# One expert load of 1 MB issued as sixteen transfers of eight partitions

## What is computed

```python
def expert_block(args):
    xb, e = args
    return (jax.nn.silu(xb @ w1[e]) * (xb @ w3[e])) @ w2[e]
```

## Time and profile before

| | |
|---|---|
| median of 3 runs | 1543.14 us (1541.34 to 1547.56) |
| span of the profiled execution | 1541.4 us |
| TensorE busy, whole span | 1370.1 us, 89% |
| share of the 16 DMA engines, 1160 to 1500 us | 1.0 |
| moved in that stretch | 144.77 MB, 426 GB/s |
| last expert load issued, landed | 1497.8 us, 1526.5 us |

### The profile page before, as it was taken

One profiled execution on the slowest core, in us unless ns is written; L12 is line 12 of the kernel. 1 busy time (PEld: TensorE's weight loads), 2 busy tenths in 40 slices (PEclk: granted clock), 3 DMA queues, 4 the chain that ended last, 5 costly groups with the idle time before them and its releaser, 6 DMA issues.

```text
span 1541.4 us, 24552 instructions
## 1 busy us (share of the span) xinstructions
PE 1370.1 (89%) x10275; PEld 1036.7 (67%) x10275; DVE 699.0 (45%) x1272; ACT 511.9 (33%) x946; POOL 66.2 (4%) x74
## 2 busy tenths in 40 slices
PE   6999999999999999999999999999996676667654
PEld 3765668887878787757999999899753333333332
DVE  4336546675545444675656657676521101011011
ACT  4426433222122223555444444555420100100001
POOL 1040010000000010101000000000000000000000
PEclk9999999999999999999999999999998977887787
DMA  8990316545854443716665359246999999999995
GB/s 339 411 302 1 152 67 249 189 142 197 293 176 147 130 147 108 216 32 249 213 213 184 130 183 306 84 143 274 419 425 425 427 426 424 426 426 425 427 425 232
DMA packets 160075, 392.39 MB, mean 255 GB/s; under 512 B 11589, under 2 KB 124761, under 8 KB 126298
## 3 DMA queue, kind: packets, MB, share of 16 engines
q1 hardware_dynamic: 159386, 389.34, 66.4%
q10 hardware_dynamic: 576, 1.44, 0.2%
HBM read 389.71 MB, written 1.05 MB: 254 GB/s over the span
## 4 chain that ended last, share of the span: by engine, by line
PE 64%; DMA 25%; ACT 4%; DVE 4%; issue 2%; SPq 1%; DVEq 0%; ACTq 0%
DMA R<-in_w_dram 23%; PE ps L1071 15%; PE ps L1072 15%; PE ps L1079 15%; PE ps L3145 3%; PE ps L1122 2%; PE ps L670 2%; PE ps L1116 2%; PE ps L1117 2%; DMA R<-in_w_ada_dram 2%; PE ps L1572 1%; PE ps L1549 1%; PE ps L1517 1%; PE ps L1636 1%; PE ps L3195 1%
## 5 line engine op out<-in xcount | busy, mean ns | idle before, releaser
L1039 DVE TENSOR_TENSOR WL<-R,WH 128x1024 fp32r<-128x1024 f32 (+1 forms) x201 | 225.1, 1137 | 163.4 <-ACT WH L1029 163.4
L3145 PE MATMUL ps<-R,XG 128*32 128x256 f32 x2032 | 170.0, 493 | 117.5 <-DMA R<-in_w_dram 111.6
L1071 PE MATMUL ps<-HH,WH 128*128 128x256 f32 (+2 forms) x872 | 272.1, 334 | 0.0
L1072 PE MATMUL ps<-HL,WH 128*128 128x256 f32 (+2 forms) x872 | 268.7, 329 | 0.0
L1029 ACT ACTIVATE WH<-R 128x1024 fp32r<-128x1024 f32 (+1 forms) x201 | 189.9, 961 | 139.0 <-PE ps L1079 105.5
L3145 PEld LDWEIGHTS ps<-R,XG 128*32 128x32 f32 x2032 | 85.0, 137 | 196.8 <-issue 179.6
L1071 PEld LDWEIGHTS ps<-HH,WH 128*128 128x128 f32 (+1 forms) x872 | 163.2, 187 | 25.5 <-issue 8.6
L1072 PEld LDWEIGHTS ps<-HL,WH 128*128 128x128 f32 (+1 forms) x872 | 163.8, 188 | 16.5
L1079 PE MATMUL ps<-HH,WL 128*128 128x256 f32 (+2 forms) x872 | 164.9, 331 | 0.0
L1071 PE MATMUL ps<-GH,WH 128*128 128x512 f32 (+1 forms) x480 | 154.2, 340 | 1.4 <-ACT WH L1029 1.4
L1072 PE MATMUL ps<-GL,WH 128*128 128x512 f32 (+1 forms) x480 | 153.4, 339 | 0.0
(11 more groups left out here) (511 smaller groups left out, 1725.3 us busy)
## 6 DMA issues: line engine op xcount, KB each, us to landing
R<-in_w_dram SPq DMA_DIRECT2D x191, 1024.0 KB, 26.5
R<-in_w_ada_dram SPq DMA_DIRECT2D x72, 1024.0 KB, 8.1
R<-in_w_gate_up_dram SPq DMA_DIRECT2D x40, 1024.0 KB, 6.5
R<-in_w_in_dram SPq DMA_DIRECT2D x20, 1024.0 KB, 7.9
R<-in_w_down_dram SPq DMA_DIRECT2D x16, 768.0 KB, 4.3
R<-in_w_down_dram SPq DMA_DIRECT2D x16, 640.0 KB, 4.1
R<-in_w_in_dram SPq DMA_DIRECT2D x8, 512.0 KB, 7.5
R<-in_w_out_dram SPq DMA_DIRECT2D x16, 256.0 KB, 8.1
```

The lines of the kernel that those rows point to most:

```text
L1039: last = e.tensor_tensor(L, w, H.bitcast(F32), ALU.subtract)
L1071: e.matmul(b[0:n, 0:N], H[:, k, 0:n], xh(k, N), start=(begins and k == ks[0]), stop=False)
L1072: e.matmul(b[0:n, 0:N], H[:, k, 0:n], xl(k, N), start=False, stop=False)
L3145: mm = e.matmul(PS[4][32 * g:32 * g + 32, 0:256], x[:, 4 * hf + k, :], w[g // 2](k)[:, 256 * (g % 2):256 * (g % 2) + 256], start=(hf == 0 ...
```

## The change

Load number 174 of 192 is issued as 16 transfers of 8 partitions (64 KB each) in place of one of 128 partitions (1 MB). All sixteen fill the same slot from the same DRAM rows, add 16 each to the slot's semaphore, and follow each other on SP's queue with no wait between them. The count at which the load has landed rises from 16 to 256 above the slot's former count. The other 191 loads are issued as before.

```diff
+    NARROW, PIECES = order.index((N_EXP - 3, 0)), 16
+
     def more_load(l, k):
 
         src, kn = expert_view(*order[l])
         landed_at = d_ring[k] if k < SLOTS else d_more[k - SLOTS]
-        load = Load(k, latest[k].landed + 16, lambda e, k: e.dma_start(fm(R[k][:, :], kn), src).then_inc(landed_at, 16))
+        parts = PIECES if l == NARROW else 1
+
+        def fill(e, k):
+            n = 128 // parts
+            for x in range(parts):
+                e.dma_start(fm(R[k][n * x:n * x + n, :], kn), src[n * x:n * x + n]).then_inc(landed_at, 16)
+
+        load = Load(k, latest[k].landed + 16 * parts, fill)
         load.after, latest[k] = latest[k], load
```

## The result

The changed kernel takes 1553.27 us (median of 4 runs, 1551.97 to 1555.58) against 1544.49 (4 runs of the kernel before beside it, 1541.34 to 1547.56). The ratio is 1.0062, with a 95% interval of 1.0047 to 1.0077: slower, by 9.6 us (7.3 to 11.9) by that ratio; the two medians lie 8.8 us apart. The forecast was 1544.6, in the range 1541.3 to 1549.0.

What follows compares the result with a forecast made beforehand. It took the experts to be bound by a load stream with full DMA engines. Extra rows added 1.5 us, issues and wait 0, to a span of 1541.4; with 1.7 from span to median, 1544.6 us, range 1541.3 to 1549.

Steps and rivals of the forecast that it cites:

- Bytes, and which engines: Load 174: every piece runs on the same eight engines, whose 8 extra rows cost 2.46 us; the other eight run ahead.
- What reaches the end: Last load's landing: extra rows move it 0, 0.5 or 2.46 us, by which engines take the pieces; 1.5 us taken.
- SP's time: SP's queue at load 174: sixteen issues take 5.6 to 9.8 us against 2.1, covered by queued loads; cost 0.
- The wait, the slot, the work behind the last load: TensorE's one wait to a higher count costs 0; load 174's slot isn't refilled; 14.9 us behind the last landing stay untouched.
- The held issues: Rival: each piece holds SP about 2.15 us, load 175 reaches idle engines; 9 to 11 us, about 1553; chance 0.10.
- The queue that counts: Rival: SP's queue holds about 11 transfers of any size, pieces crowd loads out; 1.3 to 3.2 us, about 1545.5; chance 0.08.
- the spread pieces: Rival: load 174's pieces spread over all 16 engines or changing eights, no extra bytes; 0, 1543.1 us; chance 0.10.
- a DMA share of 1.0: Sign: shares of 1.0 through 1475 to 1500 us mean right; a hole or 0.5 there means a rival.

Runs made afterwards that it cites:

- t1: Kernel before, with only partitions 0 to 63 of load 174 moved, in 8 pieces of 8 partitions 4 apart: 1543.88 us, ratio 1.0003.
- t2: Kernel before, with only partitions 64 to 127 of load 174 moved, in 8 pieces of 8 partitions 4 apart: 1548.51 us, ratio 1.0033.
- t3: Kernel before, with only partitions 64 to 127 of load 174 written, in 8 pieces, from the DRAM rows of 0 to 63: 1548.99 us, ratio 1.0032.
- t8: Kernel before, with only partitions 0 to 63 of load 174 moved, in 8 pieces of 8 neighbouring partitions: 1547.26 us, ratio 1.0024.
- t4: Kernel before, with the whole of load 174 moved as 8 transfers of 16 neighbouring partitions: 1550.32 us, ratio 1.0044.
- u1: Kernel before, with load 174 as two transfers of 64 neighbouring partitions: 1550.21 us, ratio 1.0041.
- u2: Kernel before, with load 174 as four transfers of 32 neighbouring partitions: 1552.35 us, ratio 1.0048.
- e4: Kernel before, with load 174 as two 128-partition transfers (6 KB, 1.5 KB each) and sixteen of 8 partitions with 512 B: 1545.78 us, ratio 1.001.
- t6: Kernel before, with loads 162 and 174 each split into 16 transfers of 8 neighbouring partitions: 1559.72 us, ratio 1.0109.
- t7: Kernel before, with load 3 in place of 174 split into 16 transfers of 8 neighbouring partitions, queue not yet full: 1543.52 us, ratio 0.9998.
- e1: Kernel before, with load 174 in 16 pieces of 8 partitions 4 apart, in both SBUF and DRAM: 1552.96 us, ratio 1.006.
- e2: Kernel before, with load 174 in 16 pieces written to partitions 4 apart, read from 8 neighbouring DRAM rows: 1551.15 us, ratio 1.0049.
- e3: Kernel before, with load 174 in 16 pieces written to 8 neighbouring partitions, read from DRAM rows 4 apart: 1552.47 us, ratio 1.0052.
- t5: Kernel before, with load 174 as 8 transfers of 16 partitions, 8 apart over the whole height: 1549.22 us, ratio 1.0042.

## Why the prediction was wrong

**The cause.** While rows of the narrow transfers pass, the rows of 8 KB in the stream take 0.52 us on average in place of 0.31, and from 1480 to 1495 us the stream moves 234 to 282 GB/s in place of 426. Shown: the place in SBUF decides (t1 against t2 and t3), and which partitions go together (t1 against t8); the eight engines aren't needed (t4, u1, u2), the issues aren't the cause (e4), each such load pays (t6), and only in a full stream does the kernel pay (t7). Argued: that a load of 128 partitions gives each engine its own place in SBUF, and that a transfer of fewer deals its rows over the same engines in another way, so that they write where others write.

**Bytes, and which engines (the step that failed).** The number of engines and of rows was right: 112 small packets more show eight engines. But the sum priced the load by counting rows on an engine, each at 2.46 / 8 = 0.31 us, and so could only find 8 extra rows or none. It had no term for a row that takes longer. That term is the larger one: t4, u1 and u2 have no extra rows and cost 0.41 to 0.48%, 6.3 to 7.4 us. In the changed kernel the rates give 6.8 us. That the other eight skip the load and so run ahead held against the first eight, but they were slowed as well: nearly every row of the stream was slow, which is why the rate fell to about half and not to three quarters.

**What reaches the end.** The term of 0 to 2.5 us for the extra rows held. The last engine's lag behind the mean grew from 4.3 to 6.1 us, by 1.8, where the forecast took 1.5; e1, e2 and e3, which have the extra rows too, lag by 5.5 to 6.4. The same view of t4, then of u1, then of t6:

```profile
1517.40:1533.50 16.10, 8.98 (x134) 4.65 (x132) 1.81 (x5) 2.65 (x5) 0.00 (x0) 1.00 0.74 309
1518.60:1534.70 16.10, 11.00 (x171) 5.56 (x160) 1.81 (x5) 3.28 (x6) 0.00 (x0) 1.00 0.78 329
1527.10:1543.20 16.10, 9.86 (x130) 4.98 (x130) 1.81 (x5) 2.46 (x5) 0.00 (x0) 0.89 0.50 209
```

Without extra rows (t4, u1) the lag is 4.2 and 3.5 us, no more than in before, though both kernels are slow. With two split loads (t6) it is 8.0, 3.7 over before. That is what comes out if the pieces use the same engines each time and the last engine is one of them. The times of whole runs can't tell this: 1.0062 less 1.0044 (t4) is 2.8 us, and the two intervals overlap.

**SP's time.** Right in kind, a little short in size: 11.3 us for the sixteen against 5.6 to 9.8. The median issue was 0.57 us and the longest 3.2. It was covered, as forecast: in stretches of 5 us the DMA share never fell below 0.98. e4 held SP longer, at a cost of 0.1%.

**The wait, the slot, the work behind the last load.** Right. The last load's landing carries the whole effect.

**The held issues (rival of 1553).** Its number was right and its mechanism was absent. It needed load 175 issued at 1490.8 and engines without work; load 175 was issued at 1471.4 and no engine lacked work. A forecast of 1553 for that reason would have been a hit without a reason.

**The queue that counts, and the spread pieces.** Both fell: e4 put 18 transfers in the queue at 0.1%, and t4's transfers, which do spread over all sixteen engines with no extra bytes, cost 0.44% where the rival gave 0.

**What would have shown it.** The prediction took a DMA share of 1.0 as the sign of a right forecast. The share stayed at 1.0 through the loss. It was the wrong column: an engine that is held inside a transfer counts as busy. The price of a row was taken from rows in which every transfer had 128 partitions, and nothing in the trace of before prices a narrow transfer of long rows in a full stream. Its transfers of 64 partitions (eight for each of the two layers) have rows of 256 B; the first eight are issued from 39.4 to 43.9 us into full engines (share 1.01 from 40 to 44 us). What follows from 48 to 50 us, 329 GB/s at a share of 1.08, is a stretch of small packets, most under 2 KB, and says nothing of rows of 8 KB. So the range should have had a wide upper end: with twice the time per row for only four loads of the stream, 4 x 2.46 = 9.8 us, it would have reached 1553.

**Left open.** Why all sixteen engines slow down alike, also those that by this reading write where no one else does. Why the slow stretch lasts some 18 us, the time of seven loads, for the rows of one. Why 2 x 64 costs as much as 8 x 16, where only the order of the rows differs, and why the lowest rates are alike, though narrower pieces have fewer places to write to. And which engine moves which row.

## What to carry to other kernels

In a stream that bounds the kernel, keep each transfer at all 128 partitions and cut it, if it must be cut, along the bytes of a partition; the cut in e4 (6 KB, 1.5 KB and a narrow sixteenth) cost 0.1%, the cut of a load into two partition halves 0.4%. Read GB/s beside the share of the DMA engines: a full share at half the rate is a loss that the share hides. Where the engines have gaps and nobody waits for the load, narrow pieces cost nothing (t7), though the load itself comes in at 98 GB/s. Pieces of 8 partitions 4 apart in the low half cost nothing either (t1); that each engine then writes its usual place is the reading above.

## What the runs showed of the hardware

- One load of 192 in pieces adds 6 to 10 us to a stream in which a load takes 2.46 us. It slows the loads queued around it: 0.52 us for a row of 8 KB in place of 0.31, mean of all rows from 1480 to 1496 us.
- The lowest rate in stretches of 2 us is near half of 426 GB/s for every width: 209 for sixteen pieces of 8 (193 in e3), 213 for 8 x 16 (188 in t5), 221 for 4 x 32, 213 for 2 x 64.
- Pieces of 8 neighbours with no other load beside them move 98 GB/s (t7).
- Where narrow rows are read in DRAM makes no difference that shows: t2 and t3 are 1.0033 and 1.0032.
- Transfers of 512 B rows to 8 partitions are issued in a median of 0.57 us into the full queue and 18 transfers held SP for 17 us without an engine going idle.
- The Trainium skill ("DMA: Bandwidth & Descriptors", "Rules for kernel authors") says of two transfers to disjoint partition halves: "Don't bother — they serialize". u1 agrees that there is nothing to gain, and adds a loss of 0.41% of the kernel for one such pair.
